# Down projection of a SwiGLU block as seven Strassen products of halves, with GpSimd adding the weight quarters

## What is computed

```python
h = rmsnorm(x, norm_ffn[l])
gu = h @ ffn_w_gate_up[l]                       # 1024 -> 2 * 2816
x = x + (silu(gu[..., :D_FF]) * gu[..., D_FF:]) @ ffn_w_down[l]   # 2816 -> 1024
...
return rmsnorm(x, final_norm)
```

## Time and profile before

| | |
|---|---|
| Time, median of 3 runs | 1078.31 us (1076.4 to 1078.4) |
| Span of the profiled execution | 1077.6 us, mean granted TensorE clock 0.991 |
| Around the span | the runs' times, 1076.4 to 1078.4 us, lie from 1.2 us below to 0.8 us above it |
| TensorE busy | 1042.8 us, 97% |
| VectorE, ScalarE, GpSimd busy | 522.1, 380.0 and 135.0 us |
| DMA | 87.18 MB, mean 81 GB/s |
| First down matmul, last down matmul | 946.77 us, 1066.22 us |

### The profile page before, as it was taken

How to read it: one execution, slowest core, us unless ns; L and a number is a source line. 1 busy time by engine, 2 the same in 40 slices (tenths; PEclk the granted TensorE clock), 3 DMA queues, 4 the chain that set the end, 5 groups by cost and what they waited for, 6 DMA issues and landing times.

```text
span 1077.6 us, 14413 instructions
## 1 busy us (share of the span) xinstructions
PE 1042.8 (97%) x5926; PEld 867.7 (81%) x5926; DVE 522.1 (48%) x731; ACT 380.0 (35%) x570; POOL 135.0 (13%) x207
## 2 busy tenths in 40 slices
PE   8999999999989998999999999999999999999995
PEld 7889798856678897888888888778888888888884
DVE  6775446567666788464251525453333333322313
ACT  6535545654432212442232312343222222311312
POOL 4000000525763231000000000000000000000201
PEclk9999999999999999999999999999999999999998
DMA  8322320000100013114232336323333333233201
GB/s 294 127 80 87 117 69 2 1 1 11 21 12 1 2 40 118 59 40 137 78 106 70 118 98 215 98 63 94 95 101 89 107 82 113 79 117 109 90 17 78
DMA packets 104001, 87.18 MB, mean 81 GB/s; under 512 B 13110, under 2 KB 93698, under 8 KB 103937
## 3 DMA queue, kind: packets, MB, share of 16 engines
q1 hardware_dynamic: 102288, 81.80, 25.1%
q0 software_dynamic: 1488, 4.40, 1.1%
q10 hardware_dynamic: 160, 0.07, 0.0%
HBM read 83.64 MB, written 2.62 MB: 80 GB/s over the span
## 4 chain that ended last, share of the span: by engine, by line
PE 93%; DVE 4%; ACT 1%; issue 1%; DMA 0%; POOL 0%; DVEq 0%; ACTq 0%; POOLq 0%
PE psum L901 24%; PE psum L902 24%; PE psum L903 24%; PE psum L1206 2%; PE psum L1213 2%; PE psum L1226 1%; PE psum L1305 1%; PE psum L1361 1%; PE psum L1180 1%; PE psum L1349 1%; PE psum L1278 1%; PE psum L1335 1%; PE psum L1166 1%; PE psum L1100 1%; PE psum L1029 1%
## 5 line engine op out<-in xcount | busy, mean ns | idle before, releaser
L1975 DVE TENSOR_TENSOR w_lo<-w_raw,w_hi 128x2048 fp32r<-128x2048 f32 (+2 forms) x81 | 167.5, 2068 | 232.5 <-ACT w_hi L1518 232.5
L901 PE MATMUL psum<-hT_hi,w_hi 128*128 128x512 f32 (+1 forms) x712 | 278.1, 391 | 2.1 <-DVE hT_lo L2019 1.0
L903 PE MATMUL psum<-hT_hi,w_lo 128*128 128x512 f32 (+1 forms) x712 | 277.2, 389 | 0.0
L902 PE MATMUL psum<-hT_lo,w_hi 128*128 128x512 f32 (+1 forms) x712 | 277.0, 389 | 0.0
L1518 ACT ACTIVATE w_hi<-w_raw 128x2048 fp32r<-128x2048 f32 (+2 forms) x82 | 141.4, 1725 | 157.2 <-PE psum L903 145.0
L901 PEld LDWEIGHTS psum<-hT_hi,w_hi 128*128 128x128 f32 (+1 forms) x712 | 133.2, 187 | 31.3 <-issue 2.3
L903 PEld LDWEIGHTS psum<-hT_hi,w_lo 128*128 128x128 f32 (+1 forms) x712 | 133.2, 187 | 28.2
L902 PEld LDWEIGHTS psum<-hT_lo,w_hi 128*128 128x128 f32 (+1 forms) x712 | 133.3, 187 | 27.8
L1975 DVE TENSOR_TENSOR psum<-gate_act,psum 128x512 f32<-128x512 f32 x22 | 15.3, 696 | 119.4 <-PE psum L903 119.4
L901 PE MATMUL psum<-w_hi,act_hi 128*128 128x512 f32 x176 | 68.5, 389 | 0.0
L902 PE MATMUL psum<-w_lo,act_hi 128*128 128x512 f32 x176 | 68.5, 389 | 0.0
(11 more groups left out here) (311 smaller groups left out, 1577.5 us busy)
## 6 DMA issues: line engine op xcount, KB each, us to landing
w_raw<-in_w_in_dram SPq DMA_DIRECT2D x23, 1024.0 KB
w_raw<-in_ffn_w_gate_up_dram SPq DMA_DIRECT2D x44, 512.0 KB
w_raw<-in_ffn_w_down_dram SPq DMA_DIRECT2D x10, 1024.0 KB
w_raw<-in_mem_w_kv_dram SPq DMA_DIRECT2D x4, 1024.0 KB
w_raw<-in_w_out_dram SPq DMA_DIRECT2D x4, 1024.0 KB
x_tok<-in_x_dram SPq DMA_DIRECT2D x4, 512.0 KB, 5.6
w_raw<-in_w_branch_mla_dram SPq DMA_DIRECT2D x4, 512.0 KB
w_raw<-in_w_branch_dn_dram SPq DMA_DIRECT2D x4, 512.0 KB
```

Source lines behind the costliest of these rows:

```text
L901: pe.matmul(o, s_hi, m_hi, start=first, stop=False)
L902: pe.matmul(o, s_hi, m_lo, start=False, stop=False)
L903: return pe.matmul(o, s_lo, m_hi, start=False, stop=last)
L1975: return dve.tensor_tensor(o, a, b, op)
```

## The change

The down product X (512 x 2816) times W (2816 x 1024) is cut in halves in each of its three dimensions: tokens, features (11 tiles each) and outputs. In place of eight block products there are Strassen's seven, M1 to M7, each of 256 tokens x 1408 features x 512 outputs:

- M1 = (A11+A22)(B11+B22), M4 = A22(B21-B11), M7 = (A12-A22)(B21+B22), M5 = (A11+A12)B22;
- M2 = (A21+A22)B11, M3 = A11(B12-B22), M6 = (A21-A11)(B11+B12).

They run in two groups. A step s takes one pair of feature tiles, i and i + 11. Steps 0 to 10 serve the first four products (8 banks), steps 11 to 21 the last three (6 banks). M1, M4, M7 and M5 are added to the quarters of `x1` between the groups' steps on VectorE (`take`), each sum twice where two quarters need it.

- **Weights**: a step loads three quarters' tiles of 128 x 512 (256 KB each) into `dw[s % 3]` with three DMAs on SyncE. `dw[0]` and `dw[1]` lie on `w_raw`, `dw[2]` on the start of `hT_hi`. GpSimd makes three sums (first group) or two (second). ScalarE then rounds four factors, 128x2048 (three, 128x1536) into `w_hi`, VectorE makes `w_lo`.
- **Activations**: gate/up runs through the features in pairs (`GU_ORDER`). VectorE writes the product of silu and up tile straight to SBUF (`acts`). GpSimd makes five sums of 128x256 per pair. A step rounds four factors of 256 tokens, 128x1024 (three, 128x768), into `a_hi` (three buffers, two of them on `hT`'s space); VectorE makes `a_lo`.
- **Order**: step 0's splits stand before the last gate tile's silu; step 1's wait for the last gate/up matmul, since they write into `hT`'s space and the last `w_hi`. Step s may write `w_hi` when TensorE has finished step s - 2. The load of step s may start when `w_lo` of step s - 3 is made. The last two steps are issued product by product, so that M2 and M3 are done before M6.
- **End**: `y_out`, `fin_w` and `square4` move into freed parts of `acts`; `final_norm` is loaded by GpSimd behind the sums of step 9; the squares and multiplications follow the new order of finished quarters. Each tile is still squared, scaled and stored as before.

```diff
+NP = NF // 2
+GU_ORDER = [i + NP * u for i in range(NP) for u in range(2)]
+STEPS = 2 * NP
+FINAL = [(half, 2 * row + t) for half, row in ((0, 0), (0, 1), (1, 0), (1, 1)) for t in range(2)]
+FIRST_FOUR, LAST_THREE = (1, 4, 7, 5), (2, 3, 6)
...
+        acts = v("acts", [P, NP, 7, 256], 0)
+        sums_at = [(v0 + 77 * KB), hbase + 12 * KB, hbase + 20 * KB]
+        a_hi = [at(f"a_hi{i}", [P, 4, 256], F32R, o) for i, o in enumerate(sums_at)]
+        a_lo = [at(f"a_lo{i}", [P, 4, 256], F32R, o + 4 * KB) for i, o in enumerate(sums_at)]
+        dw = [at(f"dw{i}", [P, 6, 512], F32, o) for i, o in enumerate((ring, ring + 12 * KB, hbase))]
+        late = lambda i: acts[:, i, 3:7, :].rearrange("p a b -> p (a b)")
+        y_out = [late(t) for t in range(NT)]
+        fin_w, square4 = late(NT), late(NT + 1)
...
+        NB = len(blocks)
+        def step_in(s):
+            return (w_hi[(NB + s) % 2], w_lo[(NB + s) % 2], a_hi[s % 3], a_lo[s % 3])
+        def step_sums(s):
+            return 3 * min(s + 1, NP) + 2 * max(s + 1 - NP, 0)
+        def step_free(eng, s):
+            if s < 2:
+                filled(eng, ("u", GU_ORDER[NF - 2 + s]))
+            elif s - 2 == NP - 1:
+                filled(eng, ("M", FIRST_FOUR[-1], 1))
+            else:
+                eng.wait_ge(step_used, s - 1 - (s - 2 > NP - 1))
+        factors = lambda s: 4 if s < NP else 3
...
+            for s in range(STEPS):
+                if s < 2:
+                    sp.wait_ge(w_lo_done, NB - 1 + s)
+                elif s == 2:
+                    filled(sp, ("u", GU_ORDER[NF - 1]))
+                else:
+                    sp.wait_ge(dw_lo, s - 2)
+                i = s % NP
+                places = ((4, i, 0), (5, NP + i, 0), (3, NP + i, 1)) if s < NP else ((0, i, 0), (4, i, 1), (5, NP + i, 1))
+                for unit, f, half in places:
+                    sp.dma_start(dw[s % 3][:, unit, :],
+                                 ffn_w_down[0][f * P:(f + 1) * P, 512 * half:512 * half + 512]).then_inc(dw_landed[s % 3], 16)
...
+                sp.dma_start(ot[t], y_out[t]).then_inc(out_stored, 16)
...
+            def pair_sums(i):
+                for u in range(2):
+                    released(pool, ("u", i + NP * u))
+                a = lambda n: acts[:, i, n, :]
+                pool.tensor_tensor(a(4), a(0), a(3), ALU.add).then_inc(act_sums, 1)
+                pool.tensor_tensor(a(5), a(0), a(1), ALU.add).then_inc(act_sums, 1)
+                pool.tensor_tensor(a(6), a(1), a(3), ALU.subtract).then_inc(act_sums, 1)
+                pool.wait_ge(act_sums, 5 * i + 3)
+                pool.tensor_tensor(a(1), a(2), a(3), ALU.add).then_inc(act_sums, 1)
+                pool.wait_ge(act_sums, 5 * i + 4)
+                pool.tensor_tensor(a(2), a(2), a(0), ALU.subtract).then_inc(act_sums, 1)
+            def weight_sums(s):
+                w = lambda n: dw[s % 3][:, n, :]
+                pool.wait_ge(dw_landed[s % 3], 48 * (s // 3 + 1))
+                if s < NP:
+                    pool.tensor_tensor(w(0), w(4), w(3), ALU.add).then_inc(dw_sums, 1)
+                    pool.tensor_tensor(w(1), w(5), w(4), ALU.subtract).then_inc(dw_sums, 1)
+                    pool.tensor_tensor(w(2), w(5), w(3), ALU.add).then_inc(dw_sums, 1)
+                else:
+                    pool.tensor_tensor(w(1), w(4), w(5), ALU.subtract).then_inc(dw_sums, 1)
+                    pool.tensor_tensor(w(2), w(0), w(4), ALU.add).then_inc(dw_sums, 1)
+            for i in range(NP - 1):
+                pair_sums(i)
+            for s in range(2):
+                weight_sums(s)
+            pair_sums(NP - 1)
+            for s in range(2, STEPS):
+                weight_sums(s)
+                if s == 9:
+                    pool.wait_ge(a_lo_done, NT + 1)
+                    pool.dma_start(fin_w, final_norm.partition_broadcast(P)).then_inc(fin_landed, 16)
...
+            for n, (half, t) in enumerate(FINAL):
...
+                pool.wait_ge(x2_ready, n + 1)
+                pool.tensor_tensor(y_out[t][:, c], x1[:, t, c], fin_w[:, c], ALU.mult).then_inc(xw_ready, 1)
...
-            for f in range(NF):
+            for f in GU_ORDER:
...
-            for half in range(2):
-                for f0 in range(0, NF, 4):
-                    name = ("down", half, f0)
-                    need(name)
-                    if half == 0:
-                        released(pe, ("u", min(f0 + 4, NF) - 1))
-                    wh, wl = hi(name), lo(name)
-                    for t in range(NT):
-                        key = ("down", half, t)
-                        if f0 == 0:
-                            claim(pe, key)
-                        for f in range(f0, min(f0 + 4, NF)):
-                            m = product(bank(key), act_hi[:, f, t * P:(t + 1) * P], act_lo[:, f, t * P:(t + 1) * P],
-                                        wh[:, f - f0, :], wl[:, f - f0, :], f == 0, f == NF - 1)
-                        if f0 + 4 >= NF:
-                            m.then_inc(full(key), 1)
-                    if f0 + 4 < NF:
-                        m.then_inc(w_part_used, 1)
+            def down_product(s, m, a_unit, w_unit):
+                wh, wl, ah, al = step_in(s)
+                c = slice(512 * w_unit, 512 * w_unit + 512)
+                first, last = s % NP == 0, s % NP == NP - 1
+                for t in range(2):
+                    key = ("M", m, t)
+                    if first:
+                        claim(pe, key)
+                    r = slice(t * P, (t + 1) * P)
+                    ins = product(bank(key), ah[:, a_unit, r], al[:, a_unit, r], wh[:, c], wl[:, c], first, last)
+                    if last:
+                        ins.then_inc(full(key), 1)
+                return ins
+            def step_ready(s):
+                pe.wait_ge(dw_lo, s + 1)
+                pe.wait_ge(a_lo_done, s + 1)
+            for s in range(STEPS - 2):
+                step_ready(s)
+                for m, a_unit, w_unit in ((1, 1, 0), (4, 0, 1), (7, 3, 2), (5, 2, 3)) if s < NP else ((2, 1, 0), (3, 0, 1), (6, 2, 2)):
+                    ins = down_product(s, m, a_unit, w_unit)
+                if s != NP - 1:
+                    ins.then_inc(step_used, 1)
+            for m, a_unit, w_unit in ((2, 1, 0), (3, 0, 1), (6, 2, 2)):
+                for s in (STEPS - 2, STEPS - 1):
+                    if m == 2:
+                        step_ready(s)
+                    down_product(s, m, a_unit, w_unit)
...
+            def step_split(s):
+                wh, _, ah, _ = step_in(s)
+                n = factors(s)
+                step_free(act, s)
+                act.wait_ge(dw_sums, step_sums(s))
+                A(wh[:, 0:512 * n], dw[s % 3][:, 0:n, :].rearrange("p a b -> p (a b)")).then_inc(dw_hi, 1)
+                act.wait_ge(act_sums, 5 * (s % NP + 1))
+                first = 3 if s < NP else 0
+                A(ah[:, 0:n, :], acts[:, s % NP, first:first + n, :]).then_inc(a_hi_done, 1)
+            for n, f in enumerate(GU_ORDER):
...
+                if n == NF - 1:
+                    step_split(0)
...
+                if n >= 2:
+                    released(act, ("u", GU_ORDER[n - 2]))
+                ins = A(gate_act[:, n % 2, :], bank(("g", f)), ACT.Silu)
...
+            def final_squares(n):
+                half, t = FINAL[n]
+                act.wait_ge(x2_ready, n + 1)
...
+                A(y_out[t], y_out[t], scale=rstd[:, t:t + 1]).then_inc(y_ready[t], 1)
+            for s in range(1, STEPS):
+                step_split(s)
+                if s == 18:
+                    for n in range(2):
+                        final_squares(n)
...
+            for n in range(2, 8):
+                final_squares(n)
+                if n == 6:
...
+            def step_split(s):
+                wh, wl, ah, al = step_in(s)
+                n = factors(s)
+                dve.wait_ge(dw_hi, s + 1)
+                tt(wl[:, 0:512 * n], dw[s % 3][:, 0:n, :].rearrange("p a b -> p (a b)"), f32(wh[:, 0:512 * n]),
+                   ALU.subtract).then_inc(dw_lo, 1)
+                dve.wait_ge(a_hi_done, s + 1)
+                first = 3 if s < NP else 0
+                tt(al[:, 0:n, :], acts[:, s % NP, first:first + n, :], f32(ah[:, 0:n, :]), ALU.subtract).then_inc(a_lo_done, 1)
+            for n, f in enumerate(GU_ORDER):
...
+                if n == NF - 1:
+                    step_split(0)
...
+                in_two = lambda ap: ap.rearrange("p (a b) -> p a b", a=2)
+                dst = acts[:, f % NP, 0:4, :].rearrange("p (a u) b -> p u a b", u=2)[:, f // NP]
+                tt(dst, in_two(gate_act[:, n % 2, :]), in_two(bank(key)), ALU.mult).then_inc(free(key), 1)
+            def take(m, row, half, op, step):
+                for t in range(2):
+                    key = ("M", m, t)
+                    filled(dve, key)
+                    c = x1[:, 2 * row + t, 512 * half:512 * half + 512]
```

(39 more changed lines are left out.)

72 lines of the change are left out of this document (11 added, 61 removed).

## The result

The changed kernel takes a median of 1093.92 us (1091.88 to 1095.13, four runs) beside 1077.96 for the kernel before on the same chip: a ratio of 1.0145 with a 95% interval from 1.0128 to 1.0162. Its profiled execution took 1094.61 us of device time; its span is 15.2 us longer than the one before. The forecast was 1096.

What follows compares the result with a forecast made beforehand. TensorE, busy 97% of the span, was taken as the bound. Stalls of 32.2 us less 15.0 saved gave +17.2; with 0.3 for the tail and 1 for the clock, 1077.6 became about 1096 us (forecast 1089 to 1102; 8 in 10: 1084 to 1106).

Steps and rivals of the forecast that it cites:

- turns: Down product: VectorE instructions on two SBUF operands and GpSimd's SBUF reads exclude each other, overlapping about 0.12 us per handover.
- (a): Start of the down product: late splits of step 1, pair sums and weight sums delay step 2 by 7.3 us.
- (b): Nine steps, 2 to 11: each takes 6.85 us by occupation against 5.44 of matmuls, +12.7 us.
- (c): Change of groups: VectorE's ten PSUM additions stand ahead of split 12, which makes step 12 late, +3.6 us.
- (d): Eight steps, 12 to 20: each needs 4.78 us against 4.08 of matmuls, +5.6 us.
- (e): Step 21: needs w_hi's buffer of step 19, and only six matmuls can go before, +3.0 us.
- tail: After the last matmul: the tail stays, but ScalarE takes the last squares one root later, +0.3 us.
- (f): Granted clock: TensorE's waits lower it, mostly hidden in the first group; +1 us, between 0 and 8.5.
- rival 1: Down stage: no turns, GpSimd's additions overlap the splits; stalls 11.4 against 15.0 saved, 1074.3 us; chance 0.07.
- Rival 4: GpSimd's additions in the down steps: cheaper turns, 1.04 us each, 11.6 less, 1085 us; chance 0.14.
- Rival 2: Down stage: nothing in the way at all, the whole 15 us saved, 1063 us; chance 0.02.
- rival 3: Down steps: short waits lower the clock (8.5 more) or handovers have no overlap (9.6 more), 1105 us; chance 0.13.

Runs made afterwards that it cites:

- e1: Changed kernel with GpSimd's weight sums replaced by constant fills of the same tiles, so the product is not the reference's; 1081.99 us, ratio 1.0039.
- e10: Changed kernel without four of VectorE's ten PSUM additions at the change of groups, so one quarter is not the reference's; 1092.47 us, ratio 1.0147.
- e11: Changed kernel, nothing left out, with GpSimd's output multiplications waiting for the a_lo of step 21; 1095.36 us, ratio 1.0164.
- e8: Changed kernel with a third pair of w_hi and w_lo buffers in the second group, nothing left out; 1093.05 us, ratio 1.014.
- e5: Changed kernel with weight sums mostly on VectorE (GpSimd makes those of steps 12 to 14) and a third w_hi/w_lo pair; 1077.66 us, ratio 0.9997.
- e7: Changed kernel with one GpSimd weight addition a step, waiting for a_lo of step s-2; other sums left out, product not the reference's; 1077.86 us, ratio 1.0009.
- e9: e5 with activations split before weights, last pair's sums on VectorE, GpSimd's weight sums behind step 1 only for 12 and 13, M7 first; 1073.82 us.
- e12: e9 with GpSimd's output multiplications also waiting for the w_lo of step 21; 1070.82 us, ratio 0.9939.

## Why the prediction was right, step by step

What it rests on held: TensorE was the bound, the 66 matmuls went at 0.2267 us each, and from then on the pair of VectorE and GpSimd sets the pace by turns. The stage came out at 135.9 us for 138. Some of that closeness is luck, as the terms below miss in both directions. Against the span: 1077.6, less 1.7 that don't belong to the change (gate/up ended that much earlier; the granted clock was 0.83 between 220 and 230 us in the execution profiled before, 1.00 in this one), plus 16.2 for the stage and 0.7 for the tail, gives 1092.8.

| term | forecast, us | measured, us |
|---|---|---|
| (a) start | +7.3 | 18.39 - 10.88 = +7.5 |
| (b) nine steps | +12.7 | 60.75 - 48.96 = +11.8 |
| (c) change of groups | +3.6 | 7.08 - 4.08 = +3.0 |
| (d) eight steps | +5.6 | 40.12 - 32.64 = +7.5 |
| (e) step 21 | +3.0 | 2.67 - 1.36 = +1.3 |
| tail | +0.3 | 11.83 - 11.15 = +0.7 |
| (f) clock | +1 | inside the rows above: 4.0 of spacing |

(a) Right, for the reasons given: splits of step 1 late, pair sums and weight sums in a row. e1 shows that 5.1 of it stay when the weight sums are fills.

(b) Right in mechanism, 0.9 too much. Counted as occupation, a step is 6.85; measured 6.75, with the low clock inside the first of them (7.94). The 6.75 is a mean: TensorE did not wait in nearly every step, as I had written, but before every second one (steps 4, 6, 8, 10), and steps of 5.5 us alternate with steps of 6.8 to 8.0. The turns set the mean; the pattern fits the loop of two buffers, from the end of step s-2 to step s, but that is argued. e1 (3.7 left) shows most of the term to be turns and GpSimd's longer work. Handovers with 0.12 us of overlap are borne out: 3.34 = 2.33 + 1.29 less a start 0.14 later and some 0.14 of overlap.

(c) Right in size: step 12 starts 8.07 us after the slot of group one's last matmul (1023.19), for the 8.1 forecast; 1.0 of it stands in row (b). The cause is read from the timeline and not shown by an experiment: step 11 took 4.50 us both without four of the additions (e10) and with all ten (e11).

(d) and (e) Right in sum (8.6 for 8.8), wrong in their parts. The sum left out GpSimd's first two output multiplications, which met step 20's splits and moved 1.8 us from the last wait to step 19. e11, without them, gives 6.0 and 3.1. The step that failed is "the tail stays" for a part of GpSimd's work that had moved ahead into the steps. In the second group there are two limits close together, turns (4.78) and the two-buffer loop lengthened by one addition before `a_lo`: e8 and e5 tell them apart.

(f) Right that most of it hides, at a size that differs from one execution to the next. The changed kernel's profile has one fall of the clock. In those of e10 and e11 waits of 2.0 to 2.3 us, which the changed kernel has too, brought it down twice more in the first group: the nine steps grew by 1.9 us, and step 11 fell by 2.6. Why the same wait does so in one execution and not in another was not tried.

The rivals: rival 1 (no turns) is out, by the durations and by e1. Its own arithmetic was 6 us too low: e1 has 5.1 at the start for its 2.8, 3.7 in the nine steps for 0.8 and 3.2 in the eight for 1.2, with 4.2 us of spacing in them that it had left out. Rival 4 is out: alone, an addition took 1.28 to 1.30 us in e7 and e9. Rival 2 asked for a stage with no waits; e12 comes to within 8 us of it, with other buffers and orders. Of rival 3, the clock falls behind short waits in some executions (e10, e11), but most of that hides; its handovers without overlap are out, by the 0.14 us above.

## What to carry to other kernels

Before work is given to an idle engine, look at what its operands share with the engines on the critical loop: here the additions given to GpSimd, at 13% busy before, made VectorE's `a_lo` nearly twice as long (2244 ns for 1226), since both read two SBUF tiles. If it must stay there, its place counts more than its amount: let it go behind the last split of a step, not when its load lands (9.7 us here). And an experiment that takes a delay away needs its neighbours' timelines beside it: e10 seemed to price one that was gone in e11 too. Last, a saving of TensorE work pays only after the loop that feeds it is shorter too: seven products became faster than eight, 1070.8 against 1077.5 us, when sums, buffers and the order of the splits were rebuilt around them.
